# Mean squares of the query and key heads from two rounded matmuls in place of one float32 matmul

## What is computed

```python
def rms_norm(x, g):
    xf = x.astype(jnp.float32)
    y = xf * lax.rsqrt(jnp.mean(xf * xf, axis=-1, keepdims=True) + EPS)
    return y * g.astype(jnp.float32)
...
    q = rms_norm(q.reshape(B, S, DSA_HEADS, DSA_HEAD_DIM), q_norm_g)
    k = rms_norm(k.reshape(B, S, DSA_HEADS, DSA_HEAD_DIM), k_norm_g)
```

## Time and profile before

| what | us |
|---|---|
| median of 3 runs | 1116.15 |
| lowest and highest | 1115.44, 1116.46 |
| profiled execution, span from first to last instruction | 1114.0 |
| TensorE busy in it | 1086.1 (97%) |
| VectorE, ScalarE, GpSimd busy | 564.6, 333.4, 266.1 |

### The profile page before, as it was taken

How to read it: one execution, slowest core, us unless ns; L and a number is a source line. 1 busy time by engine, 2 the same in 40 slices (tenths; PEclk the granted TensorE clock), 3 DMA queues, 4 the chain that set the end, 5 groups by cost and what they waited for, 6 DMA issues and landing times.

```text
span 1114.0 us, 12908 instructions
## 1 busy us (share of the span) xinstructions
PE 1086.1 (97%) x5042; PEld 679.3 (61%) x5042; DVE 564.6 (51%) x1042; ACT 333.4 (30%) x598; POOL 266.1 (24%) x176
## 2 busy tenths in 40 slices
PE   6999999999999999999999999999999999999998
PEld 5777788777778887878887843333333333333333
DVE  4432697488870343338996373333333333333334
ACT  6354733333342455551124211111111111111111
POOL 7433344233153344353434010000000000000000
PEclk9999999999999999999999999999999999999999
DMA  7523333224141322236368599999999999999994
GB/s 193 135 77 75 76 76 76 57 60 111 39 114 38 95 57 57 57 97 205 87 214 317 202 377 425 425 421 425 425 426 424 425 423 424 426 424 425 424 422 197
DMA packets 121692, 263.36 MB, mean 236 GB/s; under 512 B 11808, under 2 KB 97824, under 8 KB 104992
## 3 DMA queue, kind: packets, MB, share of 16 engines
q1 hardware_dynamic: 117888, 255.75, 61.4%
q0 software_dynamic: 2352, 4.18, 1.1%
q10 hardware_dynamic: 1392, 2.62, 0.6%
HBM read 262.33 MB, written 4.20 MB: 239 GB/s over the span
## 4 chain that ended last, share of the span: by engine, by line
PE 96%; issue 1%; DVE 1%; DMA 1%; ACT 0%; SPq 0%; DVEq 0%
PE bank L1023 20%; PE bank L627 19%; PE bank L646 14%; PE bank L1037 10%; PE bank L876 8%; PE bank L941 4%; PE bank L1043 3%; PE bank L1044 3%; PE bank L832 2%; PE bank L1010 2%; PE bank L815 2%; PE bank L1029 1%; PE bank L748 1%; PE bank L702 1%; PE bank L762 1%
## 5 line engine op out<-in xcount | busy, mean ns | idle before, releaser
L2017 POOL TENSOR_TENSOR piece_r<-arena,piece_r 128x1024 fp32r<-128x1024 f32 x84 | 202.5, 2419 | 309.8 <-ACT piece_r L1177 309.8
L627 PE MATMUL bank<-piece_r 128*128 128x512 f32 x936 | 232.2, 398 | 0.0
L1023 PE MATMUL bank<-arena,work 128*64 128x512 f32 x1024 | 226.7, 595 | 3.3 <-issue 2.3
L627 PEld LDWEIGHTS bank<-piece_r 128*128 128x128 f32 x936 | 171.1, 188 | 40.3 <-issue 6.9
L1023 PEld LDWEIGHTS bank<-arena,work 128*64 128x64 f32 x1024 | 74.7, 137 | 138.9 <-issue 138.9
L646 PE MATMUL bank<-piece_r 128*128 128x512 f32 x672 | 156.1, 392 | 0.0
L646 PEld LDWEIGHTS bank<-piece_r 128*128 128x128 f32 x672 | 125.3, 188 | 32.0 <-issue 6.4
L1860 DVE TENSOR_TENSOR arena<-bank,arena 128x512 f32<-128x512 f32 x126 | 80.8, 684 | 104.1 <-PE bank L1044 103.7
L1177 ACT ACTIVATE piece_r<-arena 128x1024 fp32r<-128x1024 f32 x84 | 88.4, 1057 | 100.9 <-DMA arena<-w_branch_gla_in 52.0
L1885 DVE SCALAR_TENSOR_TENSOR bias<-bank,slot_sc,bias 128x256 f32<-128x256 f32 x32 | 15.5, 484 | 159.7 <-ACT bias L1409 159.7
L2092 POOL DMA_INDIRECT arena<-x_rows,idx_pair x15 | 15.0, 998 | 335.9 <-PE bank L1010 301.1
(11 more groups left out here) (265 smaller groups left out, 1158.9 us busy)
## 6 DMA issues: line engine op xcount, KB each, us to landing
arena<-w_exp_gate_in SPq DMA_DIRECT2D x29, 2048.0 KB, 28.1
arena<-w_exp_up_in SPq DMA_DIRECT2D x29, 2048.0 KB, 24.9
arena<-w_exp_down_in SPq DMA_DIRECT2D x21, 2048.0 KB, 27.7
arena<-w_in_in SPq DMA_DIRECT2D x68, 512.0 KB, 4.3
wdn_spare<-w_exp_down_in SPq DMA_DIRECT2D x11, 2048.0 KB, 29.1
arena<-w_branch_gla_in SPq DMA_DIRECT2D x8, 512.0 KB, 4.1
arena<-w_branch_dsa_in SPq DMA_DIRECT2D x8, 512.0 KB, 5.4
arena<-w_out_in SPq DMA_DIRECT2D x2, 2048.0 KB, 12.0
```

The source lines that it names most:

```text
L627: last = mm(bank[n % 2][:, :], w[:, k, :], h[:, k, :], start=(i == 0 and k == 0), stop=(i == 2 and k == K - 1))
L1023: last = mm(onto[hf * WIDE:(hf + 1) * WIDE, :], hTe[q][:, k, :], both[:, :, k, hf * HALF:(hf + 1) * HALF], start=(k == 0), stop=(k == K - 1))
L2017: Q.tensor_tensor(quarter(w_lo, q), quarter(w_raw, q), quarter(w_hi, q).bitcast(F32), ALU.subtract).then_inc(s["wlo_ready"], 1)
```

## The change

- `mean_m` gets the rounded format (1/128 is exact in it).
- Two high and two low buffers of the squares (`sq_hi`, `sq_lo`) are laid over the start of the `spare` area, which only a late expert weight uses.
- ScalarE, after squaring, waits for its own square and copies it to the rounded high part. `qk_sq_ready` now counts two for each head.
- GpSimd subtracts the high part from the square and signals `qk_sq_lo_ready`. Its loop over weight quarters is cut so that the subtraction of head j stands behind the low parts of the quarters that ScalarE has split before tile j.
- TensorE waits for the low part and does two rounded matmuls into the same bank, in place of one float32 matmul.
- A semaphore is saved elsewhere: `own_ready` counts to 2 in place of `rows_ready`. That is in a branch for experts with more than 48 tokens, and changes no instruction before it.

```diff
-        mean_m = sb("mean_m", [P, P])
+        mean_m = sb("mean_m", [P, P], F32R)
...
+        sq_parts = nc.alloc_sbuf_tensor_at("sq_parts", [P, 4 * 512], F32R, offset=spare_at)
...
+        sq_hi, sq_lo = [[sq_parts[:, 512 * (2 * i + b):512 * (2 * i + b + 1)] for b in range(2)] for i in range(2)]
...
             def mean_square(j):
-                pe.wait_ge(s["qk_sq_ready"], j + 1)
+                pe.wait_ge(s["qk_sq_lo_ready"], j + 1)
                 if j >= 1:
                     pe.wait_ge(s["qk_rms_ready"], j)
-                mm(bank[2][:, :], mean_m[:, :], sq[j % 2], start=True, stop=True).then_inc(s["qk_ms_ready"], 1)
+                mm(bank[2][:, :], mean_m[:, :], sq_hi[j % 2], start=True, stop=False)
+                mm(bank[2][:, :], mean_m[:, :], sq_lo[j % 2], start=False, stop=True).then_inc(s["qk_ms_ready"], 1)
...
                 A(sq[j % 2], bank[n % 2][:, :], ACT.Square).then_inc(s["qk_sq_ready"], 1)
+                act.wait_ge(s["qk_sq_ready"], 2 * j + 1)
+                A(sq_hi[j % 2], sq[j % 2], ACT.Copy).then_inc(s["qk_sq_ready"], 1)
                 if j > 0:
                     root(j - 1)
...
-                dve.wait_ge(s["qk_sq_ready"], j + 1)
+                dve.wait_ge(s["qk_sq_ready"], 2 * j + 1)
...
-            split_lo(3, N_SA + 2)
+            lo_end = split_through(N_Q - 1) + 1
+            split_lo(3, lo_end)
+            for j in range(2 * H):
+                split_lo(lo_end, split_through(N_Q + j) + 1)
+                lo_end = split_through(N_Q + j) + 1
+                pool.wait_ge(s["qk_sq_ready"], 2 * j + 2)
+                Q.tensor_tensor(sq_lo[j % 2], sq[j % 2], sq_hi[j % 2].bitcast(F32), ALU.subtract)\
+                    .then_inc(s["qk_sq_lo_ready"], 1)
+            split_lo(lo_end, N_SA + 2)
```

More of the change, by code:

```diff
@@ L321, in encoder_block @@
             wout_loaded wout_hi_ready mix_hi_ready mix_lo_ready acc_ready small_ready ki_evicted small_evicted ki_mean_ready ki_cen_ready ki_sq_ready
-            ki_var_ready kiT_ready wi_ps wi_ready idx_logit_ready relu_ready relu_used qk_sq_ready qk_ms_ready
+            ki_var_ready kiT_ready wi_ps wi_ready idx_logit_ready relu_ready relu_used qk_sq_ready qk_sq_lo_ready qk_ms_ready
             qk_rms_ready qk_ready bias_ready a_ready a_abs a_exp la_ready suf_ready kd_ready kdec_ready
@@ L326, in encoder_block @@
             x_again low_mix_used x_out_ready x2_ready h2_ms x2_stored x2T_ps x2T_ready lg_ps lg_taken exps_in exps_out
-            maskb_ready rank_ready counts_ready placed idx_ps idx_ready rsg_ready sel_ready last_sel_ready rows_ps first_rows slot_sc_ps slot_sc_ready rows_ready scattered_more table_zero
+            maskb_ready rank_ready counts_ready placed idx_ps idx_ready rsg_ready sel_ready last_sel_ready rows_ps first_rows slot_sc_ps slot_sc_ready scattered_more table_zero
             wr_scaled own_ready xg_T he_ready gu_ready silu_ready hid_ready hidT_ps hidT_ready
@@ L394, in encoder_block, with split_through @@
         split_behind[N_SA:N_SA + 2] = [N_DV + 4, N_DV + 4]
+        def split_through(n):
+            upto = n
+            while upto < min(n + 4, Q_END - 1) and split_behind[upto + 1] <= n:
+                upto += 1
+            return upto
         SETUP_EPS, SETUP_WSM, SETUP_IDENT, SETUP_ALL, SETUP_TOKENS = 1, 2, 3, 4, 5
@@ L1180, in before_tile @@
             def before_tile(n):
[L1182 to L1185, removed]
+                split_hi(split_through(n))
             split_hi(0)
@@ L1850, in _ @@
             st.settle()
-            V.tensor_copy(tab_more[:, :, :], tabf[:, :, :]).then_inc(s["rows_ready"], 1)
+            V.tensor_copy(tab_more[:, :, :], tabf[:, :, :]).then_inc(s["own_ready"], 1)
             dve.wait_ge(s["slot_sc_ps"], 1)
@@ L1980, in _ @@
             step(Q.memset(gaT[:, :], 1.0))
-            ones_where(mean_m[:, :], 1.0 / HD)
+            ones_where(mean_m[:, :].bitcast(F32), 1.0 / HD)
             ones_where(mean_i[:, :], 1.0 / ID)
@@ L2105, in _ @@
                 pool.wait_ge(s["xg_T"], PAIRS_E)
-                pool.wait_ge(s["rows_ready"], 1)
+                pool.wait_ge(s["own_ready"], 2)
                 for t in range(T):
```

## The result

| | before | changed |
|---|---|---|
| median of 4 runs, us | 1115.8 | 1109.9 |
| lowest and highest | 1115.42, 1116.46 | 1109.79, 1110.67 |
| profiled execution, span | 1114.0 | 1108.9 |

The ratio of the changed kernel to the one before is 0.9945, 95% interval 0.9932 to 0.9957: 5.9 us faster, where 6.0 were forecast (the interval is 4.8 to 7.6 us).

What follows compares the result with a forecast made beforehand. TensorE was taken to bound the kernel (busy 1086.1 of 1114.0 us). Fifteen heads gaining 0.86 - 0.46 = 0.40 us each, head 14 none, give 6.0: 1116.15 - 6.0 = 1110.1 us, range 1107.2 to 1113.1.

Steps and rivals of the forecast that it cites:

- What bounds the stage: Query and key stage, 198 to 320 us: TensorE busy all 122.00 us, so TensorE savings come off the end.
- The price of the product removed and of the two added: Mean square on TensorE: float32 product 0.86 us, two rounded matmuls 0.46 together, gain 0.40 for one head.
- changing over between formats: TensorE between float32 and rounded pieces: a tile after float32 work takes 0.18 us extra; no added cost booked.
- the rival with more gained: Mean square on TensorE: busy time 1.02 is the price, 0.56 per head, 9.0 us in all, 1107.2; chance 0.06.
- the rival in which the matmuls keep the float32 rate: New mean-square matmuls: two cost 2 x 0.86 per head, 13.8 us slower, 1129.9; chance 0.01.
- Head 14 gains nothing: Before the first value tile: DMA and ScalarE set the time, so head 14's 0.40 us is lost; wait about 0.6.
- The sum: Whole kernel: 15 x 0.40 = 6.0 us off, span 1114.0 to 1108.0, median 1110.1.
- the stages behind pass the gain on: Attention and experts take as long as before; expert loads, issued behind TensorE's matmuls, start earlier by what TensorE gained.
- The side work at nothing: ScalarE's 16 copies (9.9 us) and GpSimd's 16 subtractions (20.5 us) cost nothing; no wait for the low parts.
- The lock: VectorE multiply and GpSimd subtraction share an SBUF port pair, the later one blocks; no cost taken, kept for rivals.
- late states: VectorE's states for pair_kv: held multiplies stall TensorE 1.4 us in each of four groups, 1115.7; chance 0.15.
- VectorE as the bound: Query and key stage: held multiplies grow VectorE's 93.10 us to 132.8, 10.8 us slower, 1126.9; chance 0.04.

Runs made afterwards that it cites:

- the second trace: The changed kernel itself, unaltered, measured again beside the kernel before and other versions: 1109.84 us, ratio 0.9944 to the kernel before.
- the first experiment: Changed kernel with its copy, subtraction and low-part wait kept, but the mean square again one float32 product: 1115.69 us, ratio 0.9994 to the kernel before.
- the version with the high part alone: Changed kernel without the squares' low part: one rounded matmul per head, no GpSimd subtraction, copy kept; 1106.64 us, ratio 0.9912 to the kernel before.

## Why the prediction was right, point by point

**What bounds the stage.** Right. Adding and removing one matmul a head moved the stage by +3.50 and -3.39 us; adding 16 subtractions or removing 16 copies moved it by 0.06 and 0.09.

**The price of the product removed and of the two added.** Right: 0.86 and 0.228 each, a gain of 0.40 per head. From the first mark to the issue of the last value loads, 14 heads later, the changed kernel takes 307.45 - 204.44 = 103.01 us, before 313.10 - 204.25 = 108.85: 5.84 less, 0.417 a head. The forecast had 0.40 and booked nothing for changing over between formats; that term is where the 0.017 lies. Where the mean square stands directly between two rounded tiles, the tile behind it gets shorter too. Between tiles 3 and 4, on the chain before:

```profile
226.96 0.86 PE bank L748 x2
227.82 5.49 PE bank L627 x24
```

and changed:

```profile
226.34 0.23 PE bank L757
226.56 0.23 PE bank L758
226.79 5.44 PE bank L636 x24
```

That is 0.05 more for heads 2, 6 and 10 and about as much for head 15 (5.50 to 5.44). At the other heads `pair_kv` or `pair_out`, still in float32, stands in between, and the tile behind it takes 5.66 or 5.48 in both kernels. So the stage should gain 15 x 0.405 (0.86 less the pair's 0.455, which stands as 0.45 or 0.46 in the chain) + 4 x 0.05 = 6.3, and it does. The 1.02 of busy time, the rival with more gained, is refuted by the same count. So is the rival in which the matmuls keep the float32 rate.

**Head 14 gains nothing.** Right in its place and mechanism. From the issue of the loads to the first value tile it is 6.88 us before (319.98 - 313.10) and 6.91 after. The run with head 14 in float32 and the one with the loads issued earlier agree. The wait was forecast at about 0.6. Counted from the end of the two matmuls' 0.46 us (313.31 + 0.46 = 313.77) to the tile's first record (314.36) it is 0.59 (in the second trace, with its longer load, the profile's number is 0.56); the 0.43 of the profile leaves out the drain of the last matmul, which lies inside the wait. Whoever compares the two numbers should know which of them it is.

**The sum.** 15 x 0.40 = 6.0 forecast, 15 x 0.417 = 6.26 in the stage, 5.9 in the median. That the median came within 0.1 of the forecast is partly luck: the same two kernels measured again differ by 6.4. The forecast that the stages behind pass the gain on holds within the scatter of the experts' stage, below: 1.02 us longer in this pair of traces, but 0.14 shorter in the second trace of the changed kernel (720.02). The forecast of 1110.1 took over the 2.15 us between span and median; in the four runs of the changed kernel each time is 1.75 to 1.79 over its own span, so some 0.4 of that was the difference between one execution and another.

**The side work at nothing.** Right, and shown by the first experiment and by the version with the high part alone. The copies take 0.63 us (0.62 taken), the subtractions of the changed kernel 1.28 to 1.74 (1.28 taken):

```profile
L2051 POOL TENSOR_TENSOR sq_parts<-work,sq_parts 128x512 fp32r<-128x512 f32 x16 | 23.1, 1442 | 25.1 <-ACT sq_parts L1286 24.9
L1576 DVE TENSOR_TENSOR arena<-arena,work 128x512 f32<-128x512 f32 x16 | 21.3, 1332 | 0.5
```

These are groups of the changed kernel from 198 to 331 us: busy us, mean ns, idle before. The subtractions' mean of 1.44 was the one price I had too low; it cost nothing, since each ends well ahead of its use. Head 3's subtraction ends 2.8 us ahead of the weight load of its matmul (forecast: at least 0.85), head 15's 1.2 (forecast 1.4), and the states of GLA pair 3 are there 1.6 us ahead (forecast 1.2).

**The lock.** The multiply of VectorE (L1576, before L1567) grows from a mean of 1.20 to 1.33 us. Its long cases still begin inside a weight split, six of 16, with 1.14 to 2.88 us. Three begin inside a new subtraction and take 0.92 to 1.12 in place of 0.69, as here:

```profile
298.88 1.28 POOL L2051 TENSOR_TENSOR sq_parts<-work,sq_parts 128x512 fp32r<-128x512 f32 x1 [5.57 <-ACT sq_parts L1286]
...
299.59 1.12 DVE L1576 TENSOR_TENSOR arena<-arena,work 128x512 f32<-128x512 f32 x1
```

So the new subtractions do hold it up, by 1.0 us in the whole stage. How the multiplies fall against the splits matters more: the kernel with the high part alone has no subtractions, and its multiplies take 1.45,

```profile
L1575 DVE TENSOR_TENSOR arena<-arena,work 128x512 f32<-128x512 f32 x16 | 23.2, 1452 | 0.5
```

while the one with squares rounded at once, without subtractions too, has 1.00.

Both rivals that rest on the lock, late states and VectorE as the bound, fell: in none of these traces does TensorE wait in this stage for VectorE. It waits for ScalarE's high part at the first value tile, in the version with two subtractions 0.26 us for the low part, and in the one with four for GpSimd.

## What to carry to other kernels

A plain float32 matmul among rounded ones is worth splitting where TensorE is the bound and other engines are idle: here 0.86 us against 2 x 0.23, per 128 x 512. Price it by the distance of its pieces on the chain of waits, not by the busy time of its records, and look for the places where the work that gets shorter is already running against a load: there the gain turns into idle time, and what brought it back here, in the stage, was an earlier issue of that load. Side work on an idle engine is free up to the margin between its end and its use; read that margin for the tightest place, which here was the last head and not a typical one.

## What was not expected of the hardware

**The experts' stage scatters by more than the effects under study.** Its length from the start of attention to the last long piece, in fourteen traces of kernels that are the same from there on, is 720.0 to 721.5 us (720.16 before, 721.18 changed, 720.02 for the changed kernel the second time). It doesn't go with the gain: the version with the float32 product has 720.92, the one with squares rounded at once 720.86. The marks of the two first traces stay 6.1 us apart up to 944 us of the kernel before and then fall to 5.05. In the changed kernel's chain two waits stand at that place:

```profile
947.40 0.59 issue
...
952.31 0.59 issue
```

Before, the first of its long waits is at 967.08 (0.73). Over all the traces the length goes with the place of the first such wait (0.3 us or more, in the stretch behind 700 us): 588 us behind the start of attention in four traces, with lengths of 720.97 to 721.46; 592 in seven, with 720.39 to 720.99; 601 in three, with 720.02 to 720.34. The chain names no releaser for these waits. For the first one above the timeline names ScalarE (L1425), but its instruction had ended at 947.35, 0.64 us before TensorE went on, so it was something else. That they are waits for the experts' loads is my reading: the DMA is fully taken (share 1.01), but it is so in both kernels from 700 us on, where TensorE doesn't wait yet. By that reading TensorE catches up with the loads one expert sooner or later from one execution to the next; what decides it stays open. It is the 1.02 us in the comparison of the stages above, and it is why a step of 0.4 us needs the marks of the trace rather than the total.

**GpSimd and VectorE hold each other up both ways.** The earlier trace rows had shown the multiply waiting. In the changed kernel a subtraction that starts 0.1 us behind a multiply is the longer one:

```profile
306.35 0.69 DVE L1576 TENSOR_TENSOR arena<-arena,work 128x512 f32<-128x512 f32 x1
...
306.45 1.72 POOL L2051 TENSOR_TENSOR sq_parts<-work,sq_parts 128x512 fp32r<-128x512 f32 x1 [0.43 <-ACT sq_parts L1286]
```

1.72 in place of 1.28. The six subtractions of the changed kernel that take 1.61 to 1.74 all start inside a multiply, the ten of 1.28 to 1.30 don't. The page "SBUF — State Buffer" of the Trainium skill, section "Who interferes with whom", has it so: whoever issues first keeps the pair and the other blocks. By that rule, the trace agrees.
